# dt's four partial sums added by VectorE in the fifth unit instead of by a selection matmul, with another entry order, in a two-layer hybrid decoder kernel

## What is computed

```
h    = rmsnorm(x, norm_w)                 # over D_MODEL = 1024
proj = h @ W_in                           # z, xBC, dt (16 columns), q, k, v, gates, pool
dt   = softplus(dt_raw + dt_bias)         # 16 heads
cum  = cumsum(dt * a)                     # per chunk of 128 tokens
y    = [SSD(xs, dt, cum, B, C) | retention(q, k, v) | pooling(u)]
x    = x + [rmsnorm(y_ssd * silu(z)) | ...] @ W_out
```

## Time and profile before

| what | value |
|---|---|
| time, median of 3 runs | 952.84 us (952.79 to 952.85) |
| the profiled execution | 953.56 us, its span 951.8 us |
| PE busy | 939.2 us, 99% of the span |
| DVE busy | 683.3 us, 72% |
| ACT busy | 426.2 us, 45% |
| DMA | 112.56 MB, mean 118 GB/s |

### The profile page before, as it was taken

One profiled execution on the slowest core, in us unless ns is written; L12 is line 12 of the kernel. 1 busy time (PEld: TensorE's weight loads), 2 busy tenths in 40 slices (PEclk: granted clock), 3 DMA queues, 4 the chain that ended last, 5 costly groups with the idle time before them and its releaser, 6 DMA issues.

```text
span 951.8 us, 18789 instructions
## 1 busy us (share of the span) xinstructions
PE 939.2 (99%) x7942; PEld 893.0 (94%) x7942; DVE 683.3 (72%) x933; ACT 426.2 (45%) x714; POOL 43.4 (5%) x148
## 2 busy tenths in 40 slices
PE   8999999999999999999999999999999999999996
PEld 8899999999989889999999999999999988999996
DVE  6787787866996569674557877787679757786544
ACT  6432453335774145542334225533277643554243
POOL 0000111110010000000000001111101000000000
PEclk9999999999999999999999999999999999999999
DMA  7334222144334463323332442122423451652222
GB/s 278 105 113 145 67 68 67 52 119 148 97 100 164 147 226 129 129 91 113 133 124 71 135 144 59 55 67 61 169 90 117 134 197 60 225 206 69 85 72 100
DMA packets 38421, 112.56 MB, mean 118 GB/s; under 512 B 11104, under 2 KB 14048, under 8 KB 36928
## 3 DMA queue, kind: packets, MB, share of 16 engines
q1 hardware_dynamic: 38080, 110.46, 35.4%
q0 software_dynamic: 256, 0.88, 0.3%
HBM read 93.85 MB, written 17.47 MB: 117 GB/s over the span
## 4 chain that ended last, share of the span: by engine, by line
PE 86%; DVE 7%; ACT 5%; issue 1%; DMA 1%; SPq 0%; DVEq 0%; ACTq 0%
PE acc L564 25%; PE acc L566 24%; PE acc L565 24%; ACT w_hi L955 1%; PE misc L702 1%; ACT decay L1047 1%; DVE w_lo L1242 1%; PE misc L688 1%; PE misc L755 1%; DVE halo L1767 1%; PE misc L777 1%; PE acc L847 1%; PE misc L796 1%; PE misc L827 1%; ACT decay L1054 1%
## 5 line engine op out<-in xcount | busy, mean ns | idle before, releaser
L564 PE MATMUL acc<-hin,w_hi 128*128 128x288 f32 x1504 | 450.9, 300 | 0.3 <-DVE x L1688 0.3
L566 PE MATMUL acc<-hin,w_lo 128*128 128x288 f32 x1504 | 442.9, 295 | 0.0
L565 PE MATMUL acc<-hin,w_hi 128*128 128x288 f32 x1504 | 442.9, 294 | 0.0
L564 PEld LDWEIGHTS acc<-hin,w_hi 128*128 128x128 f32 x1504 | 282.1, 188 | 13.0 <-issue 11.3
L955 ACT ACTIVATE w_hi<-w_raw 128x1024 fp32r<-128x1024 f32 x119 | 125.7, 1057 | 367.8 <-PE acc L566 367.2
L565 PEld LDWEIGHTS acc<-hin,w_hi 128*128 128x128 f32 x1504 | 282.3, 188 | 0.4
L566 PEld LDWEIGHTS acc<-hin,w_lo 128*128 128x128 f32 x1504 | 282.1, 188 | 0.0
L1242 DVE TENSOR_TENSOR w_lo<-w_raw,w_hi 128x1024 fp32r<-128x1024 f32 x119 | 145.5, 1222 | 122.0 <-ACT w_hi L955 121.7
L564 PE MATMUL acc<-mix,w_hi 128*128 128x288 f32 x416 | 123.5, 297 | 1.1 <-DVE mix L1248 0.7
L566 PE MATMUL acc<-mix,w_lo 128*128 128x288 f32 x416 | 122.6, 295 | 0.0
L565 PE MATMUL acc<-mix,w_hi 128*128 128x288 f32 x416 | 122.5, 295 | 0.0
(11 more groups left out here) (223 smaller groups left out, 1058.0 us busy)
## 6 DMA issues: line engine op xcount, KB each, us to landing
w_raw<-in_w SPq DMA_DIRECT2D x119, 512.0 KB, 3.6
decay<-cum_rows SPq DMA_DIRECT2D x8, 1024.0 KB, 6.3
h<-in_ssm SPq DMA_DIRECT2D x16, 512.0 KB, 6.3
out_ssm_s<-h SPq DMA_DIRECT2D x16, 512.0 KB, 6.0
x<-in_x SPq DMA_DIRECT2D x8, 576.0 KB, 6.7
x_kept<-x SPq DMA_DIRECT2D x4, 576.0 KB, 2.8
x<-x_kept SPq DMA_DIRECT2D x4, 576.0 KB, 5.6
out_y<-x SPq DMA_DIRECT2D x8, 288.0 KB, 2.3
```

The source lines that it names most:

```text
L564: pe.matmul(out, wh, hi, start=k == 0, stop=False)
L565: pe.matmul(out, wh, lo, start=False, stop=False)
L566: return pe.matmul(out, wl, hi, start=False, stop=k == KT - 1)
```

## The change

Four things are done.

- dt: the selection matrix, ACT's copy and `dt_folded` go. `dt_scaled` moves from DVE's unit 2 to unit 4, behind `rotate`, and does five operations on 16 partitions: a copy of the first strip out of `misc`, three additions of the others, the product with the norm's factor. DT_AT becomes 4, so ACT's bias and exponential and all `dt_part` steps come a unit later.
- entry: ACT issues the transfer of the first quarter of x; on SP's queue the first half of the first weight block comes ahead of dt's weights; the second half of that block is split after x's fourth chunk instead of its second; WARM is 11.
- boundary: between the layers DVE adds the eighth square too, so `norm_sum` of layer 1 is one pair of matmuls.
- SSD sums: they stand after block k = 4 of their unit instead of k = 2.

```diff
-DT_AT = 3
+DT_AT = 4
-WARM = 16
+WARM = 11
...
+            first, rest = slice(0, KT // 2), slice(KT // 2, KT)
             sp.dma_start(vec[:, :], a["vec"][0]).then_inc(vec_in, 16)
+            sp.dma_start(w_raw[:, 0, first, :], a["w"][0][:, first, :]).then_inc(w0_in, 16)
             sp.dma_start(wdt_all[:, :], a["wdt"][0]).then_inc(dt_in, 16)
-            first, rest = slice(0, KT // 2), slice(KT // 2, KT)
-            for i in range(4):
+            for i in range(1, 4):
                 sp.dma_start(x[:, 2 * i:2 * i + 2, :], a["x"][:, 2 * i:2 * i + 2, :]).then_inc(s_x[i], 16)
-                if i == 0:
-                    sp.dma_start(w_raw[:, 0, first, :], a["w"][0][:, first, :]).then_inc(w0_in, 16)
...
-            def dt_folded():
-
-                pe.wait_ge(*of(dt_part_ok, 1))
-                for half in range(2):
-                    mm = pe.matmul(mb[0:HEADS, half, 0:HALF], fold, halves(cvt[:, 0, 0:TOK])[:, half, :],
-                                   start=True, stop=True)
-                mm.then_inc(dt_fold, 1)
-
...
             def norm_sum(at):
 
                 last = tmp[:, (KT - 1) % 2, :]
+                if at:
+                    pe.wait_ge(sq_all, at)
+                    for half in range(2):
+                        mm = pe.matmul(mb[:, 2 + half, 0:HALF], ones, halves(ssq[:, :])[:, half, :],
+                                       start=True, stop=True)
+                    mm.then_inc(nsum, 1)
+                    return
...
                     elif u == S_NORM + 3:
-                        project(u, lambda: (ssd_norm_sum(0), ssd_norm_sum(1)), 2)
+                        project(u, lambda: (ssd_norm_sum(0), ssd_norm_sum(1)), 4)
...
-                    if u == 2:
-                        dt_folded()
...
+            eng.dma_start(x[:, 0:2, :], a["x"][:, 0:2, :]).then_inc(s_x[0], 16)
             eng.preload_act_table_set("natural_log_exp_and_others")
...
-                if j == 2:
+                if j == 4:
                     eng.wait_ge(*of(s_raw[0], 16))
                     go(act(w_hi[:, 0, KT // 2:KT, :], w_raw[:, 0, KT // 2:KT, :], ACT.Copy), w_hid, 1, 0)
...
-                    if u == 0:
-                        eng.wait_ge(*of(dt_sum, 1))
-                        go(act(halves(cvt[:, 0, 0:TOK]), mb[:, 0:2, 0:HALF], ACT.Copy), dt_part_ok, 1)
...
             def dt_scaled():
 
-                eng.wait_ge(*of(dt_fold, 1))
-                eng.wait_ge(*of(n_rstd, 1))
-                settle()
-                go(V.tensor_tensor(halves(dt_raw), mb[0:HEADS, 0:2, 0:HALF], halves(rstd[0:HEADS, :]), ALU.mult),
-                   dt_ok, 1)
+                eng.wait_ge(*of(dt_sum, 1))
+                settle()
+                go(V.tensor_copy(halves(dt_raw), mb[0:HEADS, 0:2, 0:HALF]))
+                for j in range(1, 4):
+                    settle()
+                    go(V.tensor_tensor(halves(dt_raw), halves(dt_raw), mb[32 * j:32 * j + HEADS, 0:2, 0:HALF], ALU.add))
+                settle()
+                go(V.tensor_tensor(dt_raw, dt_raw, rstd[0:HEADS, :], ALU.mult), dt_ok, 1)
...
-                            if m < KT - 1:
+                            if m < KT - 1 or l + 1 < DEPTH:
                                 add_square(m, l + 1)
...
-                    if u == 2:
+                    if u == 4:
                         dt_scaled()
```

More of the change, by code:

```diff
@@ L207, in trunk @@
         tokv = place("token_vecs", [P, TILES, 96])
-        wdt_all = place("w_dt", [P, KT * DT_W + HEADS], at=tokv_at)
+        wdt_all = place("w_dt", [P, KT * DT_W], at=tokv_at)
         wdt = wdt_all[:, 0:KT * DT_W].rearrange("p (k n) -> p k n", k=KT)
-        fold = wdt_all[:, KT * DT_W:]
         gm = place("scores", [P, GROUPS, CH])
@@ L273, in trunk @@
         dt_sum = sem("dt_parts_summed", 1)
-        dt_part_ok = sem("dt_parts_read", 1)
-        dt_fold = sem("dt_folded", 1)
         dt_ok = sem("dt_scaled", 1)
@@ L292, in trunk @@
         sq_add = sem("squares_added", KT - 1)
+        sq_all = sem("last_square_added")
         nsum = sem("norm_sum", 1)
@@ L1149, in _ @@
                         go(act(na[:, :], hvec[:, 1:2], ACT.Exp))
-                    if u == 5:
+                    if u == 6:
                         eng.wait_ge(*of(dt_s2, 1))
@@ L1153, in _ @@
                         go(act(dt_l, dt_u, ACT.Ln), dt_s3, 1)
-                    if u == 8:
+                    if u == 9:
                         eng.wait_ge(*of(cum_ok, 1))
@@ L1254, in add_square @@
                 settle()
-                if j == 0:
+                if j == KT - 1:
+                    go(V.tensor_tensor(ssq[:, :], ssq[:, :], tmp[:, j % 2, :], ALU.add), sq_all, at, 0)
+                elif j == 0:
                     go(V.tensor_copy(ssq[:, :], tmp[:, j % 2, :]), sq_add, j + 1, at)
@@ L1951, in lay_out @@
     wdt[..., 0:HEADS] = w_in[:, :, dt:q].reshape(DEPTH, KT, P, HEADS).transpose(0, 2, 1, 3)
-    fold = np.tile((np.arange(P)[:, None] % DT_W == np.arange(HEADS)[None, :]) * 1.0, (DEPTH, 1, 1)).astype(w_in.dtype)
-    wdt = np.concatenate([wdt.reshape(DEPTH, P, -1), fold], axis=2)
+    wdt = wdt.reshape(DEPTH, P, -1)
     w = np.concatenate([w_in[:, :, vv:gr], w_in[:, :, q:k][:, :, rot], w_in[:, :, k:vv][:, :, rot],
```

## The result

The changed kernel takes 956.74 us (median of 7 runs, 955.32 to 957.64), the kernel before 952.84 (7 runs, 952.67 to 953.16): a ratio of 1.0038, 95% interval 1.0028 to 1.0047. That is 3.9 us slower, where 952.4 and no change were forecast; 956.74 lies above the range too. The profiled execution took 957.64 us, its span 955.9, against 953.56 and 951.8 before. So one profile against the other shows 4.1 us.

What follows compares the result with a forecast made beforehand. PE, busy 99% of the span, was taken as the bound. dt +3.9, boundary -0.96, SSD sums -1.6 and entry -1.7 sum to -0.4 us: 952.84 becomes 952.4 us, range 951.0 to 954.4, counted as no change.

Steps and rivals of the forecast that it cites:

- the stall: PE waits for late weights before unit 7 in each layer: 2.64 us, bounds 2.3 to 3.1.
- the chain: Unit 4 to unit 7: ACT's copy, DVE's turn, five operations (3.85 us), ACT's bias, then unit 7's split at 61.32.
- The matmul: dt's selection matmul removed from PE: 1.27 us won per layer.
- the boundary: Between the layers, one pair of norm-sum matmuls goes: -0.96 us, once.
- the SSD sums: Second group of sums no longer waits for the low part of its squares: -1.6 us for two layers.
- The transposes: End of dt's chain: dt_part(6) a unit later, so PE's transposes start 0.56 us later per layer, bounds 0.4 and 0.8.
- the clock behind the wait: PE's clock after the wait before unit 7: taken to stay up, so nothing in the sum.
- second rival: PE's clock falls while it stands before unit 7: 2.6 us lost per layer, 957.6 us; chance 8%.
- the entry's: Kernel start: shorter warm-up and earlier x bring dt's second pair forward, -1.7 us, bounds -2.1 and -1.2.
- The stage: Entry: the stage behind dt's second pair comes at 12.9 instead of 14.62.
- no wait before unit 7: First rival's sign: the five operations are covered and PE does not wait there; 947.1 us, chance 10%.
- The entry gives nothing: Third rival: x's first quarter lands after the shorter warm-up, PE stands early; 954.1 or 955.5 us, chance 10%.

Runs made afterwards that it cites:

- dt_only: Kernel before with only dt's part of the change (no selection matmul, five operations in unit 4, DT_AT 4); 960.08 us, ratio 1.0074.
- fill_12: Changed kernel with 12 matmuls on ones that nobody reads, ahead of PE's wait before unit 7 in both layers; 954.18 us, ratio 1.0014.
- two_less: Changed kernel without the second and third of dt's additions, so it computes something else; 950.90 us, ratio 0.998.
- two_more: Changed kernel with dt's copy out of PSUM done three times, same values; 960.94 us, ratio 1.0088.
- no_stall: Changed kernel with dt's activations on ACT and dt_part(0) on DVE one unit later, behind the weight split for unit 7; 948.47 us, ratio 0.9951.
- one_less: Changed kernel without the third of dt's additions, so it computes something else; 954.41 us, ratio 1.0016.

## Why the prediction was wrong

Most steps that were counted from rows held. The forecast had the stall in place and cause: 5.8 against 5.3 us, inside its bounds, with the chain right to 0.2 us. The matmul and the boundary came to a tenth, the SSD sums to 0.2. The transposes cost 0.7 instead of 0.56, inside their bounds too. One slip is in the upper end of the sum: with every term at its dear bound it is 954.9, not 954.4. 956.74 lies above both.

**The step that failed is the clock behind the wait, which the sum puts at nothing.** It measured +3.0 us for the two layers, the largest error of the sum. The forecast had it as its second rival, at 8%, on the argument that from 944 to 948 "PE was busy for 0.75 of 4 us and the clock stayed at 1.00, an idleness longer than 2.64". The argument looks for the fall inside the pause. Two later stretches of that same trace show why that is no test:

```profile
948.50:949.00 0.50, 0.00 (x0) 0.00 (x0) 0.24 (x1) 0.00 (x0) 0.00 (x0) 1.00 1.07 373
949.00:949.50 0.50, 0.00 (x0) 0.00 (x0) 0.00 (x0) 0.00 (x0) 0.00 (x0) 0.75 1.08 378
```

There the clock fell at about 949.25, 4.3 us after PE's last row ended (944.93). In layer 0 of the changed kernel it fell 3.7 us after PE stopped, when PE had been at work again for 1.0. A clock that is still at 1.00 when a pause ends shows nothing about what the pause costs. The rival's mechanism came true, but not its point that "it decides at the length of idleness at which the clock falls": a wait of 2.7 us cost the clock in one layer of dt_only and not in the other. And its price was too high: the clock was lower for 3.4 us, not 5, and a fall cost 1.5 us, not 2.6. The median run has two falls, 3.0 us; fill_12 gave 2.6 back.

**The second step that failed is the entry's.** The other 1.8 us (952.4 forecast, 954.18 with the clock kept) are 0.5 of the wait, 0.3 of the transposes, and a remainder of 1.0, which fits the entry: its runs gave 0.7 instead of 1.7. The stage came where it was forecast; it is the base that was off. The profiled execution of before took 953.56 us, 0.7 more than the median, and I moved the sum to the median as if the 0.7 lay somewhere else. dt_only has the old entry too, and in its trace the same stage stands 0.6 earlier than the 14.62 of the earlier trace rows:

```profile
14.04 0.40 PE L564 MATMUL acc<-mix,w_hi 128*128 128x288 f32 x1
```

There 19 records of the warm-up lie between 4.9 and 6.9 us, where the profile of before has 11: PE was at the higher level some 2 us sooner. So the old entry differs by 0.6 between these two executions, and the profile that I counted from has the later one. Against 14.04 the mean of 12.96 is worth 1.1; why the medians give only 0.7 stays open.

The step also overlooked a bound that the change brings. dt's weights now stand a place later on SP's queue, and DVE multiplies them at 5.9 to 6.5 us instead of 3.5 to 3.7, so in the ten traces dt's first pair starts at 6.6 at the earliest. Where the warm-up ends sooner, PE waits for them, in two_less and two_more for 0.7 us. The first of them:

```profile
PE misc L574 <- DVE w_dt L1278: 0.7, 1, 0.7
```

The other rivals: "no wait before unit 7" did not happen, but no_stall shows the condition it needed, ACT's answer off DVE's path, rather than operations at a third of their length; with the transposes still late it forecast 947.1, and 948.5 was measured. "The entry gives nothing" lies nearer in the runs (0.7) than its 10% said. Its sign, a pause of PE between the warm-up and dt's first pair, is not in the changed kernel's own trace; in five others with this entry it is (0.2 to 0.7 us), but the wait is for dt's weights and not for x.

## What to carry to other kernels

Work put on one engine between two turns of a tight loop holds up the loop for its own length and for any answer that it asks of another engine: put the waiting half behind the loop's next turn, which here was worth 8.3 us with the same five operations. A wait on a TensorE that is busy 99% is to be priced with the clock behind it: look at the stretch after the wait, and not only at the wait. And when one profiled execution lies off the median, ask which term of the sum holds the difference before moving the sum across.

## What was not expected of the hardware

The clock falls late and, as far as these runs show, by chance. In the changed kernel it fell 3.7 us (layer 0) and 4.0 us (layer 1) after PE had stopped, with PE running again, and rose after 3.4 us at 1.2 GHz. Over the seven falls behind a wait in the traces it came 1.9 to 4.9 us after the stop: once inside the wait (two_more), once as it ended (one_less, layer 0), five times with PE at work again for 0.6 to 1.4 us. By the reading of the times above, waits of 1.1 us never cost it, those of 1.9 did in 12 of 20, those of 2.7 in 11 of 14, those of 4.2 in 8 of 8. The Trainium skill (TensorE: Matmul & The Clock Gate, Part 1) says that the window in which the gate watches PE's activity is free-running and does not start over with the kernel. By that, the same wait can cost the clock in one layer and not in the next, and dt_only agrees (2.7 us in both layers, one fall).

Twelve dead matmuls over the wait, 2.82 us, won 2.6 us in the median while unit 7 started no earlier. So work that nobody reads paid here; taking the wait away (no_stall) paid three times as much, 8.3 us.
